# The first feed-forward layer's last four chunks go output tile by output tile, and the next norm follows tile by tile

## The reference, cut to what matters

```
x = x + even_mixer(rmsnorm(x))        # attention
x = x + swiglu_0(rmsnorm(x))          # first feed-forward layer: gate/up, then down
x = x + odd_mixer(rmsnorm(x))         # recurrent block: gate branch, conv, RG-LRU scans
x = x + swiglu_1(rmsnorm(x))
out = rmsnorm(x)

swiglu(h):  gu = h @ w_gate_up;  (silu(gu[:, :2816]) * gu[:, 2816:]) @ w_down
odd_mixer(h):  proj = h @ w_in   # 1024 columns of gate branch, 1024 of u
               u = conv_width_4(u) + b;  gates r, i = sigmoid(u @ block weights + b) ...
rmsnorm(x): x * rsqrt(mean(x * x) + eps) * g
```

## Time and profile before

| | |
|---|---|
| median of 3 runs | 1305.33 us (1304.08 to 1308.48) |
| the profiled execution, its own time | 1305.52 us |
| its span in the profile | 1303.7 us |
| mean granted clock of PE | 0.998 of full speed |
| busy: PE, DVE, ACT, POOL | 99%, 43%, 42%, 47% |
| mean DMA traffic | 97 GB/s |

### The profile page before, as it was taken

One profiled execution on the slowest core, in us unless ns is written; L12 is line 12 of the kernel. 1 busy time (PEld: TensorE's weight loads), 2 busy tenths in 40 slices (PEclk: granted clock), 3 DMA queues, 4 the chain that ended last, 5 costly groups with the idle time before them and its releaser, 6 DMA issues.

```text
span 1303.7 us, 18386 instructions
## 1 busy us (share of the span) xinstructions
PE 1285.2 (99%) x6525; PEld 1030.1 (79%) x6525; DVE 560.3 (43%) x872; ACT 551.6 (42%) x1006; POOL 611.3 (47%) x487
## 2 busy tenths in 40 slices
PE   8999999999999999999999999999999999999998
PEld 7877777777778888888888876777888888888886
DVE  4866575756644512222202026999843131311011
ACT  5454444444434433333323246786433333333233
POOL 4565564646535444444444543530244444444442
PEclk9999999999999999999999999999999999999999
DMA  6422222222314333333332353214333333333332
GB/s 217 150 73 62 68 64 59 57 66 67 120 56 115 91 97 97 97 97 97 98 97 88 105 166 117 81 57 145 91 97 96 98 95 98 96 116 98 96 98 94
DMA packets 123415, 126.31 MB, mean 97 GB/s; under 512 B 7896, under 2 KB 106456, under 8 KB 122712
## 3 DMA queue, kind: packets, MB, share of 16 engines
q1 hardware_dynamic: 123320, 125.46, 32.1%
q10 hardware_dynamic: 32, 0.01, 0.0%
HBM read 119.15 MB, written 6.29 MB: 96 GB/s over the span
## 4 chain that ended last, share of the span: by engine, by line
PE 58%; issue 21%; POOL 12%; DVE 5%; ACT 3%; POOLq 0%; DMA 0%; SPq 0%; ACTq 0%; DVEq 0%
PE ps L1495 17%; PE ps L1497 16%; PE ps L1496 16%; POOL w_lo L495 11%; PE ps L1855 2%; PE ps L1613 1%; PE ps L1648 1%; PE ps L1625 1%; PE ps L1629 1%; PE ps L1590 1%; POOL rot L504 1%; PE ps L1659 1%; PE ps L1667 1%; DVE bkn L1139 1%; ACT w_hi L555 0%
## 5 line engine op out<-in xcount | busy, mean ns | idle before, releaser
L495 POOL TENSOR_TENSOR w_lo<-w_stage,w_hi 128x512 fp32r<-128x512 f32 (+2 forms) x430 | 543.3, 1268 | 676.8 <-ACT w_hi L555 676.4
L555 ACT ACTIVATE w_hi<-w_stage 128x512 fp32r<-128x512 f32 (+2 forms) x448 | 264.0, 594 | 582.4 <-PE ps L1497 570.0
L1495 PE MATMUL ps<-h_hi,w_hi 128*128 128x512 f32 x1104 | 439.7, 398 | 1.8 <-DVE h_lo L950 1.2
L1497 PE MATMUL ps<-h_hi,w_lo 128*128 128x512 f32 x1104 | 430.2, 390 | 0.0
L1496 PE MATMUL ps<-h_lo,w_hi 128*128 128x512 f32 x1104 | 430.1, 390 | 0.0
L1495 PEld LDWEIGHTS ps<-h_hi,w_hi 128*128 128x128 f32 x1104 | 207.3, 188 | 63.7 <-issue 17.0
L1497 PEld LDWEIGHTS ps<-h_hi,w_lo 128*128 128x128 f32 x1104 | 207.3, 188 | 43.6
L1496 PEld LDWEIGHTS ps<-h_lo,w_hi 128*128 128x128 f32 x1104 | 207.5, 188 | 43.1 <-issue 2.6
L1278 DVE TENSOR_TENSOR silu_g<-ps,rstd_wide 128x512 f32<-128x512 f32 x44 | 30.2, 686 | 327.4 <-PE ps L1497 327.4
L1495 PE MATMUL ps<-w_hi,f_hi 128*128 128x512 f32 x176 | 68.6, 390 | 0.1
L1496 PE MATMUL ps<-w_lo,f_hi 128*128 128x512 f32 x176 | 68.5, 389 | 0.0
(11 more groups left out here) (229 smaller groups left out, 1637.7 us busy)
## 6 DMA issues: line engine op xcount, KB each, us to landing
w_stage<-in_ffn_w_gate_up_dram SPq DMA_DIRECT2D x176, 256.0 KB, 3.1
w_stage<-in_ffn_w_down_dram SPq DMA_DIRECT2D x88, 256.0 KB, 2.7
w_stage<-in_even_w_in_dram SPq DMA_DIRECT2D x96, 192.0 KB, 2.5
w_stage<-in_odd_w_in_dram SPq DMA_DIRECT2D x32, 256.0 KB, 2.8
x_spill<-x_t SPq DMA_DIRECT2D x2, 2048.0 KB, 8.5
x_t<-x_spill SPq DMA_DIRECT2D x2, 2048.0 KB, 7.9
w_stage<-in_odd_w_out_dram SPq DMA_DIRECT2D x16, 256.0 KB, 2.7
w_stage<-in_even_w_out_dram SPq DMA_DIRECT2D x16, 192.0 KB, 2.4
```

The costliest lines, as they stand in the source:

```text
L495: pool.tensor_tensor(out=w_lo[:, s, 0:n], in0=stage[:, s, 0:n], in1=w_hi[:, s, 0:n].bitcast(f32), op=ALU.subtract).then_inc(chunk_lo, 1)
L555: act.activation(w_hi[:, j % RING, 0:n], stage[:, j % RING, 0:n], ACT.Copy).then_inc(chunk_hi, 1)
L1495: pe.matmul(out_, lh, rh, start=start, stop=False, skip_group_check=skip)
L1497: return pe.matmul(out_, ll, rh, start=False, stop=stop, skip_group_check=skip)
```

## The change

PE: in the second down half of the first feed-forward layer, chunks 1 to 16 stay in the loop, chunk 17 follows, and the last four chunks (18 to 21, all in the ring at once) are used output tile by output tile. The first three tiles signal `down_done`; each of the four chunks signals `chunk_used` in the fourth tile. `norm_sum(2)` moves from ahead of `("u1", 0)` to ahead of `("u0", 2)`.

DVE: `residual_by_tile` takes tiles 4 to 7 one after the other, each with its low part and its square's sum. ACT: the conversions of the first four odd chunks are no longer in `ffn`'s last `convs` but between the tiles in `second_half`; the root comes before the conversions of chunks 6 to 8.

```diff
--- before.py
+++ after.py
@@ -327,6 +327,7 @@
         turns_out = [sem("turns_out0"), sem("turns_out1")]
         pv_done, o_hi_done, o_lo_done = sem("pv_done"), sem("o_hi_done"), sem("o_lo_done")
         silu_ready, f_ready, f_hi_done, f_lo_done = sem("silu_ready"), sem("f_ready"), sem("f_hi_done"), sem("f_lo_done")
+        down_done = sem("down_done")
         lam_exp_in, lam_exp, decay_ready = sem("lam_exp_in"), sem("lam_exp"), sem("decay_ready")
         tap_done = sem("tap_done")
         pads_set, u_raw_in, u_ready, gelu_done = (sem(n) for n in ("pads_set", "u_raw_in", "u_ready", "gelu_done"))
@@ -598,17 +599,19 @@
                     square(n, 7, 8, gain)
                     conv(c0 + 5)
                 elif n == 2:
-                    highs(n, 4, 6, gain)
+
+                    square(n, 4, 6, gain)
+                    conv(c0)
+                    square(n, 6, 7, gain)
+                    convs(c0 + 1, c0 + 4)
+                    highs(n, 7, 8, gain)
+                    square(n, 7, 8)
                     conv(c0 + 4)
-                    highs(n, 6, 8, gain)
-                    square(n, 4, 6)
+                    act.activation(scratch[:, 6:7], ones[:, 0:1], ACT.Sqrt)
                     conv(c0 + 5)
-                    square(n, 6, 8)
-                    act.activation(scratch[:, 6:7], ones[:, 0:1], ACT.Sqrt)
-                    convs(c0 + 6, c0 + 8)
                     root(n)
                     act.activation(scratch[:, 4:5], ones[:, 0:1], ACT.Sigmoid)
-                    convs(c0 + 8, c0 + 9)
+                    convs(c0 + 6, c0 + 9)
                     return
                 else:
                     square(n, 4, 6, gain)
@@ -823,7 +826,7 @@
                         y_square(c)
                 else:
                     square(nn + 1, 0, 4, next_gain)
-                convs(half, half + KF)
+                convs(half, half + KF - (RING if n == 0 else 0))
 
             ffn(0, 1, G_MIX + 8)
 
@@ -1209,19 +1212,25 @@
                 dve.wait_ge(chunk_used, c_end)
                 for m, j in enumerate(tiles):
                     V.tensor_tensor(x_t[:, j, :], x_t[:, j, :], ps[:, b0 + m, :], ALU.add).then_inc(x_new, 1)
-
-                los_first = n == 2 and KD - 1 in tiles
-                if los_first:
-                    for j in tiles:
-                        x_lo_part(n, j, gain)
                 for j in tiles:
                     add_square(n, j)
-                    if not los_first:
-                        x_lo_part(n, j, gain)
+                    x_lo_part(n, j, gain)
 
             def halves(g):
 
                 return range(4 * g, 4 * g + 4)
+
+
+            def residual_by_tile(b0, c_end, n, gain):
+
+                for m, j in enumerate(halves(1)):
+                    if m < 3:
+                        dve.wait_ge(down_done, m + 1)
+                    else:
+                        dve.wait_ge(chunk_used, c_end)
+                    V.tensor_tensor(x_t[:, j, :], x_t[:, j, :], ps[:, b0 + m, :], ALU.add).then_inc(x_new, 1)
+                    x_lo_part(n, j, gain)
+                    add_square(n, j)
 
             dve.wait_ge(x_back, 16)
             for g in range(3):
@@ -1300,8 +1309,8 @@
                 if n == 1:
                     finish(C_FFN[n] + GATE_GROUPS * KD + KF)
                     return
-                for g in range(2):
-                    residual(halves(g), fb if g else 4 - fb, C_FFN[n] + GATE_GROUPS * KD + KF * (g + 1), nn + 1, next_gain)
+                residual(halves(0), 4 - fb, C_FFN[n] + GATE_GROUPS * KD + KF, nn + 1, next_gain)
+                residual_by_tile(fb, C_FFN[n] + FFN_CHUNKS, nn + 1, next_gain)
 
             ffn(0, 1, G_MIX + 8, 0)
 
@@ -1833,10 +1842,25 @@
                                 last.then_inc(y_summed, 1)
                         continue
                     tile(0, 0, True, False)
-                    with pe.Fori(0, (KF - 2) // RING) as q:
+                    with pe.Fori(0, (KF - 2) // RING - g) as q:
                         for j in range(RING):
                             tile(q * RING + (1 + j), 1 + j, False, False)
-                    tile(KF - 1, KF - 1, False, True)
+                    if g == 0:
+                        tile(KF - 1, KF - 1, False, True)
+                        continue
+
+                    tile(KF - RING - 1, KF - RING - 1, False, False)
+                    for m in range(4):
+                        for k in range(KF - RING, KF):
+                            if m == 0:
+                                chunk_ready(k + cd)
+                            s = (cd + k) % RING
+                            last = mm3(ps[:, fb + m, :], w_hi[:, s, m * P:(m + 1) * P], w_lo[:, s, m * P:(m + 1) * P],
+                                       f_hi[:, k, :], f_lo[:, k, :], False, k == KF - 1)
+                            if m == 3:
+                                last.then_inc(chunk_used, 1)
+                        if m < 3:
+                            last.then_inc(down_done, 1)
 
             ffn(0, 1, 16, 0)
 
@@ -1861,7 +1885,7 @@
                     continue
                 c = odd_chunk(stage_, k)
                 s = c % RING
-                if (stage_, k) == ("u1", 0):
+                if (stage_, k) == ("u0", 2):
                     norm_sum(2)
                 chunk_ready(c)
```

## The result

| | before | changed |
|---|---|---|
| median | 1305.29 us (9 runs, 1303.87 to 1308.48) | 1308.86 us (9 runs, 1307.49 to 1312.45) |
| ratio, 95% interval | | 1.0028 (1.0016 to 1.0040) |
| profiled execution, span | 1305.52, 1303.7 us | 1309.27, 1307.5 us |

What follows compares the result with a forecast made beforehand. PE bounds the kernel, so only its idle time and clock can be won. Terms 0.4 + 0.4 + 2.15 - 0.77 = +2.2 us took the profiled 1305.52 us to 1307.7, median 1307.5; range 1303.0 to 1310.3.

Steps and rivals of the forecast that it cites:

- The gate wait: PE's 2.71 us idle before the recurrent block's first gate step: held by ACT's queue, so it stays, gain 0.
- The second path that the text named: Norm path to the first tap: reciprocal, then `u_in` to 787.82, reaching 787.86 together with ACT's queue.
- The tail: Last four chunks tile by tile on PE: fourth chunk needed after 9 matmuls, not 36, cost +0.4 us.
- Release of the ring: Chunk 18 freed only by the tail's 39th matmul, so the first odd chunk is late: +0.4 us.
- DVE against POOL: The two engines take turns on low parts and sums, so PE waits at the norm sum: +2.15 us.
- Loads on SP's queue: Loads of chunks 8 and 9 and the spill go some 2.5 us later; ten microseconds cover it, cost 0.
- The sum: All terms together, 0.4 + 0.4 + 2.15 - 0.77: the change costs +2.2 us.
- the prediction's base: Profiled execution of the kernel before, 1305.52 us, 0.2 above the median, with the clock loss at the gate step.
- its going away: Rival: the clock no longer falls at the gate step, -1.8 us, leaving +0.4, 1305.7 us; chance 0.09.
- The forecast number: Whole kernel after the change: profiled execution 1307.7 us, median 1307.5 us.
- The point of decision of the clock: PE's idle time at which its clock falls: between 1.9 us, which kept 2.4 GHz, and 2.71, which lost it.
- its worst rival: Clock falls at the norm wait (chance 0.12, +4.0 us), here with the 3.9 us wait: +5.7 us.

Runs made afterwards that it cites:

- experiment 1: The changed kernel with first_taps(0) ahead of the conversion of chunk 9 in ACT's queue: 1304.76 us, ratio 0.9999.
- experiment 2: The kernel before with first_taps(0) ahead of the conversion of chunk 9 in ACT's queue: 1306.74 us, ratio 1.0012.
- Experiment 4: The changed kernel with chunk 4's conversion behind Sqrt's table load in ACT's queue: 1307.66 us, ratio 1.0012.
- 3: The changed kernel with norm_sum(2) put back ahead of ("u1", 0): 1306.89 us, ratio 1.0019.
- 5: The changed kernel with the tail's last four chunks used by pairs of output tiles, residuals following by pairs: 1307.69 us, ratio 1.0014.
- 10: The changed kernel with norm_sum(2) one chunk later, ahead of ("u0", 3): 1305.99 us, ratio 1.0006.
- 7: The changed kernel with its tail by pairs of output tiles and the first taps ahead of chunk 9's conversion: 1301.71 us, ratio 0.9968.
- 11: The changed kernel with norm_sum(2) ahead of ("u0", 3) and the first taps ahead of chunk 9's conversion: 1303.09 us, ratio 0.9986.
- 6: The changed kernel measured once more, unedited: 1308.93 us, ratio 1.0023 against the kernel before.
- 9: The changed kernel delayed by 13 more zero matmuls behind the last turn of x: 1309.13 us, ratio 1.0026.
- 0: The kernel before measured once more, unedited: 1305.43 us, ratio 1.0003.
- 8: The kernel before delayed by 13 more zero matmuls behind the last turn of x: 1306.82 us, ratio 1.0007.

## Why the prediction was right

**The gate wait: right.** It stayed at 2.7 us, and experiment 1 shows the cause by removing it. The second path that the text named is there too: experiment 2 shows the norm path last in the kernel before.

**The tail: right**, 0.40 us for 0.4. **Release of the ring: under-sized**, 0.68 for 0.4. ACT's conversion of the first odd chunk started 0.77 us after the start of the 39th matmul (768.02), not 0.48. The prediction took the 0.48 from the end of the second feed-forward layer. Nearer by, the last release of the old tail already took 0.76 in the trace of the kernel before; PE's last matmul of the tail, then ACT:

```profile
767.83 0.39 PE L1497 MATMUL ps<-f_hi,w_lo 128*128 128x512 f32 x1
```

```profile
768.59 0.63 ACT L555 ACTIVATE w_hi<-w_stage 128x512 fp32r<-128x512 f32 x1 [2.37 <-PE ps L1497]
```

Why it is longer isn't settled; ACT's next conversions for PE had 0.48 to 0.49 again.

**DVE against POOL: right in kind, 1.57 us for 2.15.** The sum was ready 18.9 us after the tail's start, 0.3 less than worked out, and PE came 0.3 later. Experiment 4 takes the last turn away and gets 1.1 us of the wait. The Trainium skill, page "SBUF — State Buffer", section "Who interferes with whom", says that a DVE instruction with two SBUF inputs contends with a GpSimd instruction that reads SBUF, under an exclusive lock. The sum agrees with that: 1.75 us beside POOL's `w_lo`, 0.68 without it (4).

**Loads on SP's queue: cost 0, right, but the cover was small.** The text gave it ten microseconds, from the issue of the load to its use, and left out that the load, queued behind the spill, takes 9.4 us to land (6.4 in the kernel before). The real cover was 1.6 us. In 3, 4, 5 and 10, where PE was 1.1 to 2.7 us earlier, it was gone, and the gate wait grew by 0.4 to 0.8 us.

**The sum: 1.88 us by the trace, 2.2 predicted. The median: 3.6.** The rest fits the clock at the gate step. Of 103 runs of the kernel before taken beside the experiments, 59 had a mean clock of 0.999 or more, so no fall there; of 29 runs of the changed kernel (9 + 12 + 8 delayed) none. A fall near 380 us alone doesn't explain the 29: kernels 1, 7 and 11, which have no wait at the gate step, are high in 19 of 31 runs. All three profiles of the changed kernel (with 6 and 9) show the fall at the gate step; of the three of the kernel before (with 0 and 8), two do. The times agree. The fastest runs are 1303.62 before and 1307.27 changed, 3.65 apart, and 1.88 plus the 1.70 us that a fall costs (5.37 less 3.67) are 3.58. The same 1.70 us reconciles the trace of 7 with its median (-5.25 and -3.54), and most of it for 11 (-4.14 and -2.20) and 1 (-2.49 and -0.44).

So the prediction's base had the fall in it, while more than half of that kernel's runs don't; the changed kernel seems to have it each time. The text had held the fall for the same in both, and gave a chance only to its going away. That step was wrong; its price, 1.8 us for a fall, was right. It is also by chance that the base looked typical: its profiled run had the fall, but x landed earlier in it than in any other of the 14 profiles (by 0.2 to 1.8 us), so that its 1305.52 us lay at the median. The forecast number held although nearly half of the measured 3.6 us came from a step that it had at nothing.

**The point of decision of the clock: wrong.** The text put it between a wait of 1.9 us and one of 2.7. There is no such point in the profiles. The 1.9 us wait near 380 us lost the clock in 6 of 14; a wait of 2.71 us (8) and one of 3.37 (3) kept it, and 2.71 in the changed kernel didn't. The text's range has a slip as well: its worst rival, +5.7 us, is 1311.0, not 1310.3.

Why the changed kernel falls each time isn't settled. The gate wait is as long as before. The profiles are not sorted by its place either: no fall at a gate step that starts at 795.74 (8) or 796.68 (3), a fall at 794.46, 796.58 (6) and 798.17. What may go with it is the idle time in front of the norm sum: without it, and a gate wait of 3.1 us, 6 of 11 runs are high (10). But 3, with none there and 3.4 at the gate, has 2 of 10, 4, with 0.3 and 3.2, has 1 of 12, and 5, with none and 3.5, has 0 of 12. A delay of 0.9 us did not make the kernel before behave like the changed one (8), but the gate step of 10 also lies 1.2 us earlier than the changed kernel's, so its place in time isn't excluded. The cause stays open.

## What to carry to other kernels

Before a path is shortened, list all that its consumer waits for, and read what stands ahead of each in its engine's queue. Here the first tap stood behind a weight conversion that PE releases, and the earlier norm bought nothing until two statements changed places. Using the ring's last buffers output by output asks for all of them at once and gives them back late; pairs of outputs had neither stall and still let the residuals start early. A load's cover counts from when it lands, not from when it is issued. A profiled execution has one clock history: look at the clock of all runs before its time stands for the median.

## What the runs showed of the hardware

- By when x landed, 14 executions of almost the same program stood up to 1.8 us apart near 380 us; with the clock, up to 3.4 us apart at the tail.
- After the same 1.9 us wait near 380 us the clock fell to 1.2 GHz in 6 of 14 profiles (0, 1, 2, 4, 10, 11) and stayed up in the others. The fall costs 1.6 us.
- After 3.51 us of idle time the low level lasted 6.8 us (795.4 to 802.2 in 5), after 3.49 us it lasted 3.4 (799.3 to 802.7 in 2), and after 3.37 us there was none (3). The length of a wait does not settle what the clock does.
- A DVE operation and a POOL operation with two SBUF inputs each took turns: four on POOL in 5.97 us, and each DVE one among them took 0.8 to 1.1 us longer than alone. A residual with one input in PSUM did not.
- A 256 KB load issued behind the 2 MB spill landed 9.4 to 10.0 us after its issue (changed, 3, 4, 5, 7, 10, 11).
